# Meta keys' products with V stacked in one float32r product, a fourth PSUM bank for small results, weight sums behind a head's store

## The reference

```python
h = jnp.concatenate([meta, x], axis=1)
...
for l in range(DEPTH):                      # two layers
    hn = rmsnorm(h, norm_gain[l])
    proj = hn @ w_in[l]
    dq, dk, dv, dg, fq, fk, fv, ff, fg = jnp.split(proj, split_points, axis=-1)
    ...
    do = diff_attention(dq, dk, dv, lam, chunk_ids)   # 4 heads of two maps: a = p0 - lam * p1, then a @ v
    do = rmsnorm(do, subln_gain[l], SUBLN_EPS) * (1.0 - lam_init)
    ...
    do = do * jax.nn.silu(dg)
    ...
    fo = forgetting_attention(fq, fk, fv, cum_logf, positions)   # 8 heads of width 64, decay by cum_logf
    fo = fo * jax.nn.silu(fg)
    h = h + jnp.concatenate([do, fo], axis=-1) @ w_out[l]
out = rmsnorm(h, final_gain)
```

## Time and profile before

| | |
|---|---|
| time, median of 3 runs | 2724.56 us (2722.77 to 2729.76) |
| the profiled execution | 2731.44 us, its span 2729.6 us |
| granted TensorE clock, mean over the span | 0.988 |
| TensorE products busy | 2649.7 us, 97% |
| VectorE / ScalarE / GpSimd busy | 1637.5 / 1201.0 / 466.2 us |

### The profile page before, as it was taken

How to read it: one execution, slowest core, us unless ns; L and a number is a source line. 1 busy time by engine, 2 the same in 40 slices (tenths; PEclk the granted TensorE clock), 3 DMA queues, 4 the chain that set the end, 5 groups by cost and what they waited for, 6 DMA issues and landing times.

```text
span 2729.6 us, 43070 instructions
## 1 busy us (share of the span) xinstructions
PE 2649.7 (97%) x16632; PEld 2278.5 (83%) x16632; DVE 1637.5 (60%) x2944; ACT 1201.0 (44%) x2372; POOL 466.2 (17%) x674
## 2 busy tenths in 40 slices
PE   6999999999999999999999999999998999999999
PEld 6888888888899888878777997888897788887887
DVE  5766664444535666554446366555437877778767
ACT  6444444333424444443334462223335655555444
POOL 2211232310001222452000124000013101011000
PEclk9999999999999999999999899999998999999999
DMA  4121377761312212897202423113232344444443
GB/s 150 57 67 64 120 191 198 202 158 44 142 58 74 74 64 74 245 233 182 82 24 78 129 72 114 47 47 100 93 92 95 116 127 121 124 126 153 177 154 135
DMA packets 219225, 314.21 MB, mean 115 GB/s; under 512 B 15478, under 2 KB 157494, under 8 KB 219022
## 3 DMA queue, kind: packets, MB, share of 16 engines
q0 software_dynamic: 50304, 151.30, 19.2%
q1 hardware_dynamic: 168720, 160.16, 18.6%
HBM read 267.26 MB, written 111.22 MB: 139 GB/s over the span
## 4 chain that ended last, share of the span: by engine, by line
PE 84%; DVE 6%; ACT 3%; issue 2%; DMA 2%; POOL 2%; SPq 0%; DVEq 0%; ACTq 0%; POOLq 0%
PE PS L1078 79%; PE PS L1087 5%; DMA T<-TMP 2%; DVE WL L2451 1%; DVE AL L2494 1%; POOL TMP L3427 1%; DVE ST L2623 0%; DMA R<-s_adap 0%; DVE TMP L2606 0%; POOL T L3424 0%; DVE T L2599 0%; ACT top L1881 0%; ACT TMP L1830 0%; DVE top L2636 0%; ACT TMP L1720 0%
## 5 line engine op out<-in xcount | busy, mean ns | idle before, releaser
L1078 PE MATMUL PS<-AH,WH 128*128 128x344 f32 (+2 forms) x2160 | 805.0, 373 | 23.7 <-DVE AL L2494 9.4
L1078 PE MATMUL PS<-AL,WH 128*128 128x344 f32 (+2 forms) x2160 | 756.8, 350 | 0.0
L1078 PE MATMUL PS<-AH,WL 128*128 128x344 f32 (+2 forms) x2160 | 756.3, 350 | 0.0
L1078 PEld LDWEIGHTS PS<-AH,WH 128*128 128x128 f32 x2160 | 408.8, 189 | 83.5 <-issue 21.0
L1078 PEld LDWEIGHTS PS<-AH,WL 128*128 128x128 f32 x2160 | 408.5, 189 | 36.0
L1078 PEld LDWEIGHTS PS<-AL,WH 128*128 128x128 f32 x2160 | 409.8, 190 | 32.1 <-issue 1.0
L1078 PE MATMUL PS<-WH,AH 128*128 128x256 f32 (+1 forms) x972 | 309.4, 318 | 3.7 <-DVE WL L2451 3.7
L1078 PE MATMUL PS<-WL,AH 128*128 128x256 f32 (+1 forms) x972 | 308.6, 317 | 0.0
L1078 PE MATMUL PS<-WH,AL 128*128 128x256 f32 (+1 forms) x972 | 308.6, 317 | 0.0
L2623 DVE TENSOR_REDUCE ST<-PS 128x1 f32<-128x784 f32 (+8 forms) x272 | 187.9, 732 | 143.0 <-PE PS L1078 142.5
L2451 DVE TENSOR_TENSOR WL<-W,WH 128x1024 fp32r<-128x1024 f32 x157 | 192.6, 1229 | 125.6 <-ACT WH L1708 125.5
(11 more groups left out here) (406 smaller groups left out, 4419.5 us busy)
## 6 DMA issues: line engine op xcount, KB each, us to landing
W<-in_k_w_in SPq DMA_DIRECT2D x66, 512.0 KB, 4.2
s_wt<-in_w_up POOLq DMA_DIRECT2D x96, 352.0 KB, 6.3
W<-in_w_ada SPq DMA_DIRECT2D x48, 512.0 KB, 5.2
s_wd<-in_w_down POOLq DMA_DIRECT2D x66, 256.0 KB, 6.3
W<-s_wt SPq DMA_DIRECT2D x64, 256.0 KB, 3.5
W<-in_w_in SPq DMA_DIRECT2D x28, 512.0 KB, 3.8
W<-in_w_up SPq DMA_DIRECT2D x52, 256.0 KB, 3.3
W<-in_w_out SPq DMA_DIRECT2D x24, 512.0 KB, 3.5
```

The lines of the kernel that those rows point to most:

```text
L1078: return e.matmul(out, lhsT, rhs, start=start, stop=stop, skip_group_check=True)
```

## The change

1. **Meta keys.** Two new tiles take the meta keys' operands, in float32r: `P3` for the weights, `V3` for V, each with three bands of 32 rows. `P3` holds high, low, high; `V3` holds high, high, low. One product over 96 rows then gives high x high + high x low + low x high. The transposes take 32 columns of `P` instead of 16; columns 16 to 31 are the first tokens, and a column of ones and zeros (`OF_META`) sets their rows to zero in `V3`. For heads 4 to 7 each map's product is 128 columns wide with zeros in the other map's half, and both maps add up in the bank. New steps are `pt_lo` (VectorE) for the low part of `P3`, and `v_lo` (VectorE) for that of `V3`; the eviction of a meta part makes two copies instead of one; `v_out` of group 2 makes two copies (heads 0 to 3) or four (4 to 7). The sum in the bank begins with the float32r product and goes on with the float32 ones of the full tiles.
2. **Banks.** Bank 2 joins `few`, blocked from the scores of tile 7 until their exp. The planner takes the bank that is known to be free first, and hands its choice to the kernel (`BANK_AT`).
3. **Order.** The planner's costs change for the meta products, and it plans `pt_lo` and `v_lo`; so the whole written order is made anew.
4. **Weight sums.** Where the next thing on GpSimd's list behind an `ada` store is a head's store, the weight sums due are issued behind the head's store. `gate` waits for `gate_pre` of its head.

The core of the diff:

```diff
-            V = own("V", [128, 2, 9, 128])[:, :, :, :]
+            V, V3a = own("V", [128, 2, 8, 128])[:, :, :, :], own("V3a", [128, 256], F32R)
...
+            P3 = own("P3", [128, 2, 256], F32R)
+            V3 = [V3a[:, :], own("V3b", [128, 256], F32R)[:, :]]
...
-                self.few = {b: (0, 0.0) for b in (5, 6, 7)}
+                self.few = {b: (0, 0.0) for b in (2, 5, 6, 7)}
...
             def bank(self, but=None):
-                return min((b for b in self.few if b != but), key=lambda b: self.few[b][0])
+                return min((b for b in self.few if b != but), key=lambda b: (self.few[b][1] is None, self.few[b][1] or self.few[b][0]))
...
-                    return sum(216 if t == blk[1] else 432 if t < 8 else 610 for t in tiles) + 150
+                    return sum(216 if t == blk[1] else 432 if t < 8 else 210 for t in tiles) + 150
...
                     need += [self.scored[b] for m in range(2) for b in region_banks(j, m)]
+                    if j == 7:
+                        need.append(self.few[2][1])
...
             def step_av(g, bi):
...
+                e.wait_ge(*v_lo.at(("v", l, g)))
                 for m in maps(g):
-                    for n in range(len(parts(l, g, bi))):
+                    e.wait_ge(*pt_lo.at((l, g, bi, m, 0)))
+                    for n in range(1, len(parts(l, g, bi))):
...
-                        x = mm(e, bank(b)[r0:r0 + rn, qa:nq], V[0:kr, vs, t, r0:r0 + rn], PT[0:kr, PT_SLOT[l, g, bi, m], t, qa:nq],
-                               i == 0, i == len(tiles) - 1)
+                        if t == 8:
+                            x = mm(e, bank(b)[:, 0:nq], V3[vs][0:96, 128 * m:128 * m + 128], P3[0:96, slot_, 0:nq], m == 0, meta and m == maps(g)[-1])
+                        else:
+                            qa = 128 if t == blk[1] else 0
+                            x = mm(e, bank(b)[r0:r0 + rn, qa:nq], V[:, vs, t, r0:r0 + rn], PT[:, slot_, t, qa:nq], False, i == len(tiles) - 1)
...
                     o, i = pt_evac(l, g, bi, parts(l, g, bi)[n], PT_SLOT[l, g, bi, m], b)
+                    if n == 0:
+                        e.activation(P3[64:96, PT_SLOT[l, g, bi, m], 0:i.shape[1]], i, ACT.Copy)
                     e.activation(o, i, ACT.Copy).then_inc(*pt_act.mark(key))
...
+                def step_pt_lo(g, bi, m, n):
+                    key = (l, g, bi, m, n)
+                    pt, nq, b = PT_SLOT[l, g, bi, m], NM if BLOCKS[l][bi] == (8,) else 256, banks.place.get(("pt",) + key, 0)
+                    side_ = pt_act if PT_SIDE[key] == "act" else pt_dve
+                    e.wait_ge(*side_.at(key))
+                    e.tensor_tensor(P3[32:64, pt, 0:nq], bank(b)[0:32, 0:nq], f(P3[0:32, pt, 0:nq]), ALU.subtract).then_inc(*pt_lo.mark(key))
...
+                def step_v_lo(g):
+                    vs, b = g % 2, banks.place.get(("vt", l, g, 2), 0)
+                    e.wait_ge(*v_turned.at((l, g, 2)))
+                    if g in (4, 5):
+                        e.tensor_tensor(V3[vs][0:96, 64:192], ident[0:96, :], ident[0:96, :], ALU.subtract)
+                    for (o, i), (hi, _) in zip(cols3(g, vs, 64, 96, b), cols3(g, vs, 0, 32, b)):
+                        x = e.scalar_tensor_tensor(o, i, OF_META[0:32, :], f(hi), ALU.mult, ALU.subtract)
+                    x.then_inc(*v_lo.mark(("v", l, g)))
...
             def attention(l):
...
+                own = [i for i, st in enumerate(STEPS[l]) if st[0] == "ada_out" or st[0] == "gate" and st[1] < 7]
+                store_next = {a for a, b in zip(own, own[1:]) if STEPS[l][b][0] == "gate"}
+                owed = 0
...
-                        if at_ > turns:
+                        if at_ in store_next:
+                            owed += at_ > turns
+                        elif at_ > turns:
                             weight_sums(next(sums))
...
+                        for _ in range(owed):
+                            weight_sums(next(sums))
+                        owed = 0
```

More of the change, by code:

```diff
@@ L633, in place @@
                     at["scores", g, j] = end
+                    if j == 7:
+                        self.count += 1
+                        self.few[2] = (self.count, None)
                     if j == BLOCKS[l][-1][0]:
@@ L702, in side_of @@
                         return ready, 740
+                    if n == 0:
+                        return ready, (600, 750)
                     return ready, (170 + 1.02 * wide, 250 + 0.68 * wide)
+                if what == "pt_lo":
+                    return at["hi", st[1:]], 440
+                if what == "v_lo":
+                    return at["hi", "v", st[1]], 500
                 if what == "av_out":
@@ L779, in put_side @@
                     del self.p_free[0:2]
+                    if j == 7:
+                        self.few[2] = (self.few[2][0], back)
                     for m in range(2):
@@ L808, in put_side @@
                         at["qk", st[1], st[2]] = back
+                elif what == "v_out" and st[2] == 2:
+                    at["hi", "v", st[1]] = seen
                 elif what == "v_out":
@@ L811, in put_side @@
                     at[("v",) + st[1:]] = back
+                elif what == "v_lo":
+                    self.leave(("turn_v", st[1], 2), back)
+                    at["v", st[1], 2] = back
                 elif what == "ada_out":
@@ L968, in attention_order @@
                 flush(nxt)
-            return steps, clocks.side
-        STEPS, EVICTS = zip(*(attention_order(l) for l in range(2)))
+            return steps, clocks.side, clocks.bank_of
+        STEPS, EVICTS, BANK_AT = zip(*(attention_order(l) for l in range(2)))
         for l in range(2):
@@ L1071, in build @@
         banks = Banks()
-        ALL, FEW = range(8), (5, 6, 7)
+        ALL = range(8)
         W_OVER = {}
@@ L1140, in tensor_attention, with turn_bank @@
             at_work = [None]
-            def turn_bank(key, freed_by):
-                b, free = banks.take(key, [freed_by], FEW, at_work[0])
+            def turn_bank(st, key, freed_by):
+                b, free = banks.hold(key, [freed_by], BANK_AT[l][st])
                 for c, k in free or ():
@@ L1157, in step_unit @@
                         e.wait_ge(*fill_lo.at((l, ci + 1, 7)))
-                    at_work[0], free = banks.take(key, [freed], FEW)
+                    at_work[0], free = banks.hold(key, [freed], BANK_AT[l][g, kind, ci])
                     for cc, kk in free or ():
@@ L1256, in step_tr @@
                 key = (l, g, bi, m, n)
-                b = turn_bank(("pt",) + key, (pt_act if PT_SIDE[key] == "act" else pt_dve, key))
+                b = turn_bank(("tr", g, bi, m, n), ("pt",) + key, (pt_lo if n == 0 else pt_act if PT_SIDE[key] == "act" else pt_dve, key))
                 if n == 0:
@@ L2425, in scalar, with cols3 @@
             ffn()
+        def cols3(g, vs, r0, r1, b):
+            if g < 4:
+                return [(V3[vs][r0:r1, 0:128], bank(b)[0:32, 0:128])]
+            return [(V3[vs][r0:r1, 192 * m:192 * m + 64], bank(b)[0:32, 64 * m:64 * m + 64]) for m in range(2)]
         def pt_evac(l, g, bi, part, pt, b):
@@ L2679, in step_gate @@
                         e.wait_ge(*av_out.at((l, g, len(BLOCKS[l]) - 1)))
+                    e.wait_ge(*max((gate_pre.at((l, g, "g", ci)) for ci in range(len(cols_of(l, g, "g")))), key=lambda x: x[1]))
                     e.scalar_tensor_tensor(OTt[:, c:c + n], OTt[:, c:c + n], sc, GT[:, c:c + n], ALU.mult, ALU.mult).then_inc(*gated.mark((l, g)))
@@ L3758, in layout @@
         cols[r:128:32, 20 + r % 2] = 1.0
+    for r in range(NM):
+        cols[r:128:32, 22] = 1.0
     a["k_cols"] = cols
```

68 lines of the change are left out of this document (43 added, 25 removed).

## The result

The changed kernel takes 2713.8 us (median of 5 runs, 2708.37 to 2714.26), the kernel before on the same chip 2723.95 (5 runs, 2722.04 to 2729.76). The ratio is 0.9949, 95% interval 0.9932 to 0.9965: half a per cent faster. That is inside the range, at its slow end, but the gain is some 10 to 14 us where 36 were forecast. The profiled execution took 2713.80 us, its span 2712.0.

What follows compares the result with a forecast made beforehand. TensorE, busy for 97% of the span, was taken as the bound. Meta product -37, late evictions and stage ends +3 +3, bank -5, weight sums 0 gave -36 us: 2689 us against the median 2724.56, range 2668 to 2714.

Steps and rivals of the forecast that it cites:

- The product: Meta keys times V on TensorE: 22.7 us saved in heads 0 to 3, 12.2 in 4 to 7, 2 in small blocks; 37.
- rival 2: Meta product on TensorE: 96 rows stall like 16, so only 17 us are saved: 2708 us; chance 0.14.
- rival 4: Meta product on TensorE: few rows are already cheap, 0.11 us out and 0.12 in, no gain: 2726 us; chance 0.03.
- late evictions +6: VectorE's added copies and subtractions make evictions late: +3 us of TensorE waits, +3 at the bare ends of the stages.
- the bank -5: Fourth PSUM bank for small results takes away TensorE's waits for a bank: -5 us, bounds -12 and +8.
- the new order no mean: Whole written order planned anew can shift any stall: given no mean, only room in the range.
- rival 5: Products with V wait for the last meta tile's subtraction, 72 x 0.85 = 61 us: 2744 us; chance 0.08.
- Weight sums, 0: Weight sums behind a head's store on GpSimd's queue: 0, bounds -3 and +3, since ScalarE, which waits for stores, is not the bound.
- Rival 3: TensorE is freed in the attention stages, but weight loads by DMA set the pace, no change: 2724 us; chance 0.06.
- Rival 1: More gain: bank waits go altogether (-12) and a stretch at lower clock is not entered again (-3): 2672 us; chance 0.12.

Runs made afterwards that it cites:

- leaving the side work out: Changed kernel in the same written order, without the second copy and the subtraction at the 108 meta tiles: 2701.09 us, ratio 0.9916.
- Nudges of one cost: One planner cost moved, order replanned: changed kernel, copies 830 ns for 600 (2702.2 us) or new product 150 for 210 (2704.95); kernel before, old product 550 for 610 (2765.7).
- the product in the old order: Changed kernel's product, copies and subtractions in the written order of the kernel before, three banks, weight sums in front of the store: 2769.18 us, ratio 1.0159.
- a nudge without reason: Changed kernel with the planner's cost of the float32r meta product at 150 ns instead of 210, order replanned: 2704.95 us, ratio 0.9920.

## Why the prediction was wrong

- **The product** was right in mechanism and nearly in size. Heads 0 to 3: 4.07 to 3.37 us for an undisturbed largest step, 0.70 where 0.71 was forecast; by the medians of all sizes 0.65, 20.8 us. Heads 4 to 7, medians: 4.16 to 3.83, 3.30 to 2.97, 2.44 to 2.20, 1.58 to 1.33, on average 0.29 and not 0.38, since the two products take 0.33 to 0.44 and not 0.23: 9.2 us, not 12.2. Blocks of meta queries: 0.25 each, 2 us, as taken. Together 32 of 37. Rivals 2 and 4 are out, though the time lies near rival 2's 2708: in 20 of 32 steps 0.12 us lie between the 96-row product and the next start, as between products of 128 rows, and going back to the 16-row product cost 28 us. By the Trainium skill ("TensorEngine Tiling (Array Packing)", Tiling Modes), which lists row tiles of 32, 64 and 128 rows, 96 rows were to count as the whole array; the 0.12 us agree. The four-fold rule of the Trainium skill ("TensorEngine Tiling (Array Packing)", Overview, Theoretical Speedup) did not show here, where the 16-row product had the array to itself: its two passes cost 0.83 us in the kernel before, not a quarter of 0.43.
- **The stalls: the step that failed.** The sum took over the few stalls of the old order and put three small terms on top: late evictions +6, the bank -5, the new order no mean, +1 us in all. Measured, to the same point of the program: 32.1 us of stalls before, 44.9 in the changed kernel, 13 more. With the product's 32 us that gives -32 + 13 = -19, measured -18.6 at full clock.
- **Late evictions, +6:** the sum took it that the meta tile is ready long before its product, which is so, and priced that wait and the bare ends of the stages. It named the work that is late behind them on VectorE, but not that the tile's PSUM bank stays taken for the two instructions more, and that whatever needs a bank next stands behind it. In the order of before the stalls grow by 56 us (32.1 to 88.5), near rival 5's 61, but only 8.5 of them stand in front of the products with V (4.0 to 12.5); 26 stand in front of transposes (3.5 to 29.5) and 20 in front of projections (8.0 to 28.1). In the new order with four banks, leaving the side work out brings 8 us at full clock, 9 in time: there the +6 was nearly right.
- **The bank, -5:** wrong sign by itself, with the order planned anew (+10 us, +5 at full clock). That the planner uses it to put work ahead, behind which scores then wait for exps, is my reading of the rows; no run tries it alone. With the low part it is worth 23 us in time. The forecast added what was not a sum: the bank pays for the chain that the product brings.
- **The new order, no mean:** the order of before has few stalls, and nothing said that its successor would have as few. Nudges of one cost moved the time by some 9 us down and 41 up; three nudges are too few for a mean.
- **The clock:** the forecast had it as constant. It took 5 to 8 us of the time. With more stalls goes a lower clock: from 80 us to the same point of the program, the length times what the mean clock lacks to 1.00 is 14.1 us in the profile before, 18.7 in that of the changed kernel and 29.7 with the product in the old order, at 32.1, 44.9 and 88.5 us of stalls.
- **Weight sums, 0:** right for the order of before (ratio 1.0001), 7 us in the new one (4.4 at full clock). The argument "ScalarE is not the bound" failed where ScalarE waited 11.9 us for a store: TensorE stood for 5.1 of them.
- Rival 3 (weights set the pace) is out: DMA share 1.05 in 1200 to 1250 with TensorE at 49.57 of 50 us. Rival 1 is out by its time; its bank waits went, but others came. That the time lies inside the range is luck: its slow end came from rival 2, whose mechanism did not occur.

What stays open: why an order is good, and what the held bank and the fuller VectorE cost each by itself. The changed kernel's loss to exps is seen, but no single rule removed it. The fastest version found is the changed kernel with 830 ns for the copies: 2702.2 us, ratio 0.9914; a nudge without reason did as well.

## What to carry to other kernels

An added instruction on a PSUM result can cost not only its own reader but all who want that bank: count the time for which a buffer is held. Where a written order is made anew, the few stalls of the old trace are no longer given: leave room for a loss on the new order, and try several. An edit off the critical path (the store) was worth nothing in one order and 16 us in another.

## What the runs showed of the hardware

The spread between runs of one kernel is almost wholly TensorE's granted clock: times spread over 17 us, span times clock has a standard deviation of 1.5. A stall can cost more than its length: the window above with stalls of 2.4 and 2.8 us has a clock of 0.74, the one of before at the same place, with 1.2 us of idle TensorE in all, 0.91; and behind the stall of 15 us the clock is 0.79 over 14 us in which TensorE is busy throughout. A float32r product of 96 rows over 256 columns took 0.12 us to the next start in front of a float32 product of 128 rows and columns in 20 of 32 steps, and 0.21 in front of one of 64 columns in all 32.
